# Head norm of three conv rows: a block-matrix mean, Ln and Exp on ScalarE and a Newton step on VectorE in place of group sums, a power on GpSimd and transposes

## What is computed

```python
proj = rms_norm(x, g_pre_mix) @ w_in                 # 3 x 512 conv and 3 x 512 attention columns
hc, bg, cg, q, k, v = split(proj, 6)
u = cg * hc
conv = bg * (u[s]*w2 + u[s-1]*w1 + u[s-2]*w0)        # causal, per channel, 512 channels
y_conv = conv * rsqrt(mean(conv*conv over each group of 64 channels) + 1e-6) * g_conv_out
y_attn = group_rms_norm(banded_attention(q, k, v), g_attn_out)
y = concat(y_conv, y_attn) @ w_out                   # then residual, norm, SwiGLU, residual
```

## Time and profile before

| | |
|---|---|
| time, median of 3 runs | 1108.63 us (1108.47 to 1108.7) |
| the profiled execution's own time | 1108.71 us |
| its span, first to last instruction | 1106.7 us |
| PE busy | 1096.9 us, 99% |
| DVE busy | 759.8 us, 69% |
| ACT busy | 467.3 us, 42% |
| POOL busy | 162.4 us, 15% |
| chain that ended last | PE 98%, ACT 1%, DVE 1% |
| mean granted clock of PE | 0.999 |

### The profile page before, as it was taken

The page is one execution under the profiler, slowest core; times in us unless marked ns, Lnnn a source line. Parts: engine busy times, 40 slices in busy tenths (PEclk is TensorE's granted clock), DMA queues, the critical chain, the costliest instruction groups (busy, mean ns, idle before and its releaser), DMA issues.

```text
span 1106.7 us, 15974 instructions
## 1 busy us (share of the span) xinstructions
PE 1096.9 (99%) x5653; PEld 909.5 (82%) x5653; DVE 759.8 (69%) x1206; ACT 467.3 (42%) x818; POOL 162.4 (15%) x258
## 2 busy tenths in 40 slices
PE   9999999999999999999999999999999999999997
PEld 7888888878888888888888888888888888888886
DVE  6878854354546656868787777878787786555584
ACT  6542333555555655734322232323223256444441
POOL 3300022010101220312112211211221110000031
PEclk9999999999999999999999999999999999999999
DMA  7332216300100444535546445543644689776632
GB/s 272 107 120 75 58 57 224 119 20 20 39 3 19 163 162 133 172 95 174 159 142 209 136 122 187 177 146 114 218 136 152 214 307 377 232 237 223 218 114 79
DMA packets 116182, 164.10 MB, mean 148 GB/s; under 512 B 7752, under 2 KB 73304, under 8 KB 116128
## 3 DMA queue, kind: packets, MB, share of 16 engines
q1 hardware_dynamic: 98496, 103.30, 29.3%
q0 software_dynamic: 16464, 55.89, 14.4%
q10 hardware_dynamic: 1168, 4.20, 1.0%
HBM read 119.56 MB, written 46.94 MB: 150 GB/s over the span
## 4 chain that ended last, share of the span: by engine, by line
PE 98%; ACT 1%; DVE 1%; DMA 0%; issue 0%; DVEq 0%; POOL 0%; POOLq 0%
PE psum L1278 34%; PE psum L1305 18%; PE psum L872 12%; PE psum L1111 10%; PE psum L1162 8%; PE psum L1023 4%; PE psum L915 3%; PE psum L896 2%; PE psum L886 2%; PE psum L861 1%; PE psum L999 1%; PE psum L923 0%; PE psum L1005 0%; PE psum L905 0%; ACT arena L1514 0%; PE psum L992 0%
## 5 line engine op out<-in xcount | busy, mean ns | idle before, releaser
L1278 PE MATMUL psum<-arena_r,ws 128*128 128x512 f32 x960 | 224.1, 389 | 0.0
L1278 PEld LDWEIGHTS psum<-arena_r,ws 128*128 128x128 f32 x960 | 180.3, 188 | 37.3
L1278 PE MATMUL psum<-hT,ws 128*128 128x512 f32 x720 | 169.9, 389 | 0.0
L1278 PEld LDWEIGHTS psum<-hT,ws 128*128 128x128 f32 x720 | 135.2, 188 | 27.9
L872 PE MATMUL psum<-hT,ws 128*128 128x512 f32 (+1 forms) x624 | 142.2, 380 | 0.6 <-ACT arena L1540 0.6
L1305 PE MATMUL psum<-hT 128*128 128x512 f32 (+1 forms) x600 | 135.2, 385 | 0.0
L1305 PEld LDWEIGHTS psum<-hT 128*128 128x128 f32 x600 | 111.3, 188 | 22.5
L872 PEld LDWEIGHTS psum<-hT,ws 128*128 128x128 f32 x624 | 107.9, 189 | 19.9 <-issue 0.8
L2408 DVE TENSOR_TENSOR misc<-misc,psum 128x512 f32<-128x512 f32 x100 | 68.6, 686 | 48.3 <-PE psum L1278 46.0
L1729 ACT ACTIVATE ws<-o_raw 128x512 fp32r<-128x512 f32 x40 | 25.1, 627 | 139.1 <-DVE o_raw L2386 138.6
L1162 PE MATMUL psum<-ws,hT 128*128 128x512 f32 x348 | 81.8, 393 | 0.0
(11 more groups left out here) (263 smaller groups left out, 1557.7 us busy)
## 6 DMA issues: line engine op xcount, KB each, us to landing
raw<-in_w_ffn_in SPq DMA_DIRECT2D x44, 512.0 KB, 4.2
act_scratch<-arena POOLq DMA_DIRECT2D x77, 256.0 KB, 3.2
raw<-in_w_in SPq DMA_DIRECT2D x22, 512.0 KB, 3.8
arena<-in_w_ffn_out POOLq DMA_DIRECT2D x22, 512.0 KB, 5.6
arena<-act_scratch SPq DMA_DIRECT2D x38, 256.0 KB, 3.3
arena<-in_x SPq DMA_DIRECT2D x16, 512.0 KB, 6.3
raw<-in_w_out SPq DMA_DIRECT2D x16, 512.0 KB, 3.4
raw<-act_scratch SPq DMA_DIRECT2D x26, 256.0 KB, 3.2
```

The source lines that it names most:

```text
L1278: last = mm(blocks(bank), w[:, k * P:(k + 1) * P], b_operand(i, part, k), start=fresh_bank and k == 0 and w is hi and part == 0, stop=k == ...
```

## The change

For rows 0 to 2 the means are made in channel layout. ACT squares the row into `CU` and makes its high part in `CR` (`high_sq`); DVE makes the low part (`low_sq`). PE multiplies both, in 512-column halves, by `same_head`, a 128x128 matrix with 1/64 where two channels share a group: 4 fp32r matmuls. Each of 128 partitions of `PP[2]` then holds its group's mean at each position. ACT takes Ln(mean + eps) and Exp(-0.5 x) of it (`conv_roots`), DVE does one Newton step on the inverse root and multiplies (`mix_row`), in four instructions over 1024 columns. POOL has no part in it any more, and the transposes and group sums of these rows are gone. `same_head` is filled once by ACT from `group`, in `high_sq(0)`.

```diff
             def stats(t):
 
-                pe.wait_ge(conv_sq, t + 1)
-                if t == 0:
-                    pe.wait_ge(v_copied, NT)
-                else:
-                    pe.wait_ge(conv_var, t)
-                conv_stats(PP[3]).then_inc(conv_stat, 1)
...
-            behind = {(4, 1): (stats, 0), (4, 3): (stats, 1), (4, 4): (norms, 0),
-                      (5, 0): (norms, 1), (5, 1): (stats, 2), (5, 4): (norms, 2)}
+                pe.wait_ge(conv_mixed, means_split(t))
+                if t > 0:
+                    pe.wait_ge(conv_mixed, mixed(t - 1))
+                for half in range(2):
+                    for part in (CR, CU):
+                        last = mm(PP[2][:, half * HALF:(half + 1) * HALF], same_head, row_r(part)[:, half * HALF:(half + 1) * HALF],
+                                  start=(part == CR), stop=(part == CU))
+                last.then_inc(conv_stat, 1)
+
+            behind = {(FRONT - 2, 3): 0, (FRONT - 1, 0): 1, (FRONT - 1, 3): 2}
...
+            def high_sq(t):
+
+                act.wait_ge(conv_sq, squared(t, 0))
...
+                if t > 0:
+                    act.wait_ge(conv_mixed, mixed(t - 1))
+                go(row_r(CR), row(CU), ACT.Copy).then_inc(conv_sq, 1)
+
+            def conv_roots(t, bank):
+
+                act.wait_ge(conv_stat, t + 1)
+                go(row(CR), bank, ACT.Ln, bias=eps_col[:, 0:1]).then_inc(conv_root, 1)
+                act.wait_ge(conv_root, rooted(t) - 1)
+                go(row(CR), row(CR), ACT.Exp, scale=-0.5).then_inc(conv_root, 1)
...
-            front_copy_first(4), square_y(0)
-            front_high(5, 0), square_y(1), front_high(5, 1), front_high(5, 2), front_high(5, 3)
-            spread_conv(0), front_high(5, 4), spread_conv(1), front_high(5, 6)
-            front_copy_first(5), square_y(2), front_high(5, 5)
+            front_copy_first(4), square_y(0), high_sq(0)
+            for i in range(4):
+                front_high(5, i)
+            conv_roots(0, PP[2]), square_y(1), front_high(5, 4), high_sq(1), front_high(5, 6)
+            front_copy_first(5), conv_roots(1, PP[2]), square_y(2), high_sq(2)
...
-            first_chunk(0), spread_conv(2)
+            first_chunk(0), front_high(5, 5), conv_roots(2, PP[2])
...
+            def low_sq(t):
+                dve.wait_ge(conv_sq, squared(t, 1))
+                tt(row_r(CU), row(CU), row_r(CR).bitcast(F32), ALU.subtract).then_inc(conv_mixed, 1)
+
+            def mix_row(t):
+
+                f, mean, y = row(CR), PP[2], row(CONV_ROWS[t])
+                dve.wait_ge(conv_root, rooted(t))
+                chain(stt(mean, mean, EPS, f, ALU.add, ALU.mult))
+                chain(stt(mean, mean, -0.5, f, ALU.mult, ALU.mult))
+                chain(stt(f, mean, 1.5, f, ALU.add, ALU.mult))
+                stt(y, y, params[:, t, 3:4], f, ALU.mult, ALU.mult).then_inc(conv_mixed, 1)
...
-            conv_stats_read(0)
+            low_sq(0)
             make_u3(4)
...
             front_low(5, 3)
+            mix_row(0)
             make_c22(4, tiles_of(row(CV), 1), 1)
-            conv_stats_read(1)
             front_low(5, 4)
+            low_sq(1)
             make_c21(4, tiles_of(row(CV), 0), 0)
-            conv_mix(0)
             front_low(5, 6)
             make_c12(4)
             times(2, 1, u2).then_inc(front_out, 1)
 
+            mix_row(1)
             make_u2(5)
-            conv_mix(1)
+            low_sq(2)
             make_u3(5)
-            conv_stats_read(2)
+            low(1, 0, 0)
             front_low(5, 5)
-            low(1, 0, 0)
+            mix_row(2)
             make_c22(5)
-            conv_mix(2)
```

More of the change, by code:

```diff
@@ L135, in trunk_layer @@
         arena_r = sb("arena_r", [P, NF * SEQ], F32R)
+        with nc.sbuf_tensor("misc_r", [P, 4 * BAND], F32R) as misc_r:
+            pass
         misc = sb("misc", [P, 4 * BAND])
@@ L138, in trunk_layer @@
         group = sb("group", [P, 2])
+        eps_col = sb("eps_col", [P, 1])
         params = sb("params", [P, PAIRS, 5])
@@ L242, in trunk_layer, with squared, rooted, means_split @@
         u2, u3, c22, s11, s4 = [misc[:, n * 512:(n + 1) * 512] for n in range(5)]
+        def squared(t, part):
+            return 2 * t + 1 + part
+        def rooted(t):
+            return 2 * t + 2
+        def means_split(t):
+            return 2 * t + 1
+        def mixed(t):
+            return 2 * t + 2
+        same_head = misc_r[:, 3 * 512:3 * 512 + P]
         s1, s2 = [o_raw[:, 4 * n:4 * n + 4, :].rearrange("p i c -> p (i c)") for n in range(2)]
@@ L411, in trunk_layer @@
         conv_norm = sem("conv_norm")
+        conv_root = sem("conv_root")
         conv_mixed = sem("conv_mixed")
@@ L569, in store_conv @@
             def store_conv(t):
-                sp.wait_ge(conv_mixed, t + 1)
+                sp.wait_ge(conv_mixed, mixed(t))
                 sp.dma_start(y_d[t * P:(t + 1) * P, :], row(CONV_ROWS[t])).then_inc(conv_stored[t], 16)
@@ L693, in _ @@
             pool.wait_ge(consts_made, 5)
+            nc.gpsimd.memset(eps_col[:, :], EPS).then_inc(consts_made, 1)
             chain = Chain(pool, pool_seq)
@@ L732, in conv_norm_factors @@
             def conv_norm_factors(t):
[L734 to L737, removed]
+                pool.wait_ge(conv_var, 1)
+                factors_to(crs[:, :], var[:, :], 16, conv_factors, 1)
             def o_norm_factors(t):
@@ L742, in o_norm_factors @@
                 factors_to(rst[:, :], o_eps[:, :], UNITS, o_rs, t + 1)
-            for t in range(PAIRS - 1):
-                conv_norm_factors(t)
             pool.wait_ge(prod, multiplied(FRONT - 1, 4))
@@ L969, in step @@
                     if s == 1 and t == 0:
-                        pe.wait_ge(conv_mixed, PAIRS - 1)
+                        pe.wait_ge(conv_mixed, mixed(LAST - 1))
                     if s == 2 and t > 1:
@@ L1116, in stats @@
             def stats(t):
-                pe.wait_ge(conv_sq, t + 1)
-                if t == 0:
-                    pe.wait_ge(v_copied, NT)
-                else:
-                    pe.wait_ge(conv_var, t)
-                conv_stats(PP[3]).then_inc(conv_stat, 1)
-            def norms(t):
-                pe.wait_ge(conv_rs, t + 1)
-                if t > 0:
-                    pe.wait_ge(conv_mixed, t)
-                conv_norms(PP[2], 0, NT).then_inc(conv_norm, 1)
-            behind = {(4, 1): (stats, 0), (4, 3): (stats, 1), (4, 4): (norms, 0),
-                      (5, 0): (norms, 1), (5, 1): (stats, 2), (5, 4): (norms, 2)}
+                pe.wait_ge(conv_mixed, means_split(t))
+                if t > 0:
+                    pe.wait_ge(conv_mixed, mixed(t - 1))
[5 more added lines that the diff above has]
+            behind = {(FRONT - 2, 3): 0, (FRONT - 1, 0): 1, (FRONT - 1, 3): 2}
             for n in range(FRONT):
@@ L1137, in _ @@
                     if (n, i) in behind:
-                        task, t = behind[n, i]
-                        task(t)
+                        stats(behind[n, i])
             for q in range(AHEAD):
@@ L1203, in _ @@
                     pe.wait_ge(oT_read, PAIRS)
-                    pe.wait_ge(conv_sq, PAIRS)
+                    pe.wait_ge(conv_sq, squared(LAST, 0))
                     conv_stats(PP[3]).then_inc(conv_stat, 1)
                 if c == 6:
-                    pe.wait_ge(conv_rs, PAIRS)
+                    pe.wait_ge(conv_rs, 1)
                     conv_norms(PP[3], 0, NT).then_inc(conv_norm, 1)
@@ L1458, in square_y, with spread_conv @@
                 go(row(CU), row(CONV_ROWS[t]), ACT.Square).then_inc(conv_sq, 1)
[L1460 to L1464, removed]
+            def high_sq(t):
+                act.wait_ge(conv_sq, squared(t, 0))
+                if t == 0:
+                    act.wait_ge(consts_made, 6)
+                    go(same_head.rearrange("p (g d) -> p g d", d=HD),
+                       group[:, :].rearrange("p (g o) -> p g o", o=1).broadcast_to([P, 2, HD]), ACT.Copy, scale=1.0 / HD)
+                if t > 0:
[6 more added lines that the diff above has]
+                go(row(CR), row(CR), ACT.Exp, scale=-0.5).then_inc(conv_root, 1)
+            def spread_conv():
+                act.wait_ge(conv_factors, 1)
                 go(row(CR).rearrange("p (g d) -> p g d", d=HD),
@@ L1700, in _ @@
                     act.wait_ge(oT_psum, PAIRS)
-                    spread_conv(PAIRS - 1)
+                    spread_conv()
                 for task, i in tasks.get(c, ()):
@@ L2331, in conv_last @@
             def conv_last(_):
-                dve.wait_ge(conv_norm, PAIRS)
+                dve.wait_ge(conv_norm, 1)
                 stt(row(PAIRS - 1), PP[3], params[:, LAST, 3:4], row(CV), ALU.mult, ALU.mult).then_inc(mix_done, 1)
```

## The result

The changed kernel takes 1124.91 us (median of 4 runs, 1124.46 to 1125.85) against 1108.59 us before (4 runs, 1108.47 to 1108.7). The ratio is 1.0148, 95% interval 1.0131 to 1.0166: 16.3 us slower. The forecast was 1123.7 us in a range of 1118 to 1130. The profiled execution took 1124.78 us, its span is 1122.9 us, the mean granted clock 0.991.

What follows compares the result with a forecast made beforehand. The prediction took PE as the bound: 16.75 us of new waits less 5.7 us of saved work gave +11.0, plus 4.0 for the clock, +15.0 on 1108.7, so 1123.7 us, range 1118 to 1130.

Steps and rivals of the forecast that it cites:

- What PE saves: PE, product (4, 1) to first piece: blocks replace three rows' group sums and transposes, gaining 5.7 us without any wait.
- A table load: ACT, around Ln and Exp of rows 0 to 2: six loads at 1.28 us each, plus 0.1 us lost overlap.
- the walk: Instruction lists laid on each other: PE waits 6.9, 4.0 and 5.85 us, 16.75 in all; less 5.7 gained, +11.0 us.
- The mix: DVE, each row: four dependent instructions in place of one, 4 x 1.32 = 5.3 us.
- The clock: PE after the waits of 6.9 and 5.85 us: slower clock costs 2 us each; the 4.0 us wait at 0.
- Queues and later stages: SP's stores ahead of k's weights and v's return come about as late as PE: 0; later stages have no slack.
- One sign missed: Profile sign: the distance from product (4, 1) to the first piece grows by 11 to 15 us, all else as before.
- A: Rival: the waits come as in the walk but PE's clock holds: 1119.7 us; chance 0.20.
- B: Rival: a table switch costs up to 1.4 us beyond each of six loads, 8.3 us: 1128 or 1132; chance 0.06.
- D: Rival: table loads are free beside ACT's other work, +4.3 us: 1113.0 us; chance 0.06.
- C: Rival: `mix_row` ends before PE needs what is queued behind it; 1103.0 us with all three waits gone; chance 0.04.

Runs made afterwards that it cites:

- e7: Changed kernel with ACT and DVE lists reordered, no Newton step, and Exp in place of Ln so no table loads: 1103.19 us, ratio 0.9953 to the kernel before.
- e4: Changed kernel with 60, 36 and 52 dummy transposes filling PE's three waits: 1120.35 us, ratio 1.0107 to the kernel before.
- e3: Changed kernel with the three Newton instructions of the mix left out: 1110.51 us, ratio 1.0019 to the kernel before.
- e2: Changed kernel with Ln replaced by Exp, so no table has to be loaded: 1116.16 us, ratio 1.0070 to the kernel before.
- e6: Changed kernel with ACT and DVE lists reordered and the three Newton instructions left out: 1104.93 us, ratio 0.9967 to the kernel before.
- e1: Changed kernel with the bank-emptying sums of rounds 4 and 5 ahead of the mixes on DVE: 1120.52 us, ratio 1.0106 to the kernel before.

## Why the prediction was right

- **What PE saves, 5.7 us.** Right: 5.4 us measured with a wait of 0.4 us left (e7). Blocks took 0.90 us.
- **A table load at 1.28 us.** Right: six loads of 1.28 us, in the order of the walk (the last starts at 186.79, a little behind the stretch that I gave, since the walk left the clock out), and the kernel without them is 8.75 us faster, clock included.
- **The mix, 4 x 1.32 us.** Slightly too high: 155.34 to 160.33 is 4.99 us. The three instructions of the Newton step took 1.23 us each and not 1.29. This is a part of why DVE as a whole got 13.8 us more and not the 16 that I worked out.
- **The walk.** Waits of 6.9, 4.0 and 5.85 us forecast, 6.72, 4.02 and 5.05 measured, each at the instruction named, behind the DVE line named. The third is shorter because product (5, 4) before it was slow; where it ran at full speed, in e4, the time before (5, 6) was 6.07 us.
- **The clock, 4 us.** The mechanism was right (granted clock at the lower level after the long waits, full speed in e4), and 4.6 us is its price by e4. The parts were not all right: I gave 0 to the wait of 4.0 us, with bounds of 0 to 1; it also dropped the clock and cost 0.8 us for the block on the path and 0.9 us that the next wait took in. The two priced at 2 us came to 1.9 and 2.0. That they came so close is luck: 2 us was the middle between bounds of 0 and 4, not a reading, and in e3 the same kernel paid in some runs and not in others. The rows behind the bounds were indirect as well. The windows view gives a granted clock of 1.00 for the first 10 us before the change, but only since the trace has no clock record before 9.01 us and the view counts such time as full. The spacing of the transposes bears the reading out: 0.21 us from start to start until 8.97 us, 0.11 from there on.
- **Queues and later stages, 0.** Right: 15.95 us late at the first scores and 16.2 us over the span.
- **One sign missed.** From product (4, 1) to the first piece I expected 11 to 15 us more; it is 16.1. Those bounds were the walk without and with 4 us for the clock, with no room for an error in either.
- **Rivals.** A is what e4 shows as a separate run, not the kernel itself. B and D are out by e2. C needed the mixes to end early; e6 gets there by leaving out three of four instructions and moving the one that is left.

Sum: 15.0 us forecast, 16.3 measured. Two errors partly cancel in the 1.3 us: the waits came to 1.0 us less than forecast (15.8 against 16.75), the lower clock to 1.6 us more (5.6 against 4.0); the rest, 0.4 us in the stretch and 0.2 behind it, I did not separate further. Not tried: keeping the Newton step and having it done elsewhere, or moving the blocks themselves. Nor do these runs say what the missing Newton step means for the accuracy of a use of e6.

## What to carry to other kernels

When an engine saves work on the bound, walk the new chain that replaces it, instruction by instruction against the queue in which each stands: here 5.7 us of PE work saved came with 15.8 us of waits, because two table loads and four dependent instructions on DVE stood in a chain that PE waited for, twice through a sum queued behind it. A long wait on PE should be priced above its length, since PE came back at half its clock, and what is won or lost there changes the next wait too. Moving the blocked instruction ahead only moves the wait while the chain is as long as before; shortening the chain and then ordering it is what made the kernel faster.

## What was not expected of the hardware

- Transposes of 128 columns, back to back at 0.11 us, kept the granted clock at 1.00 through stretches of 6.9, 4.2 and 6.1 us (e4), where it fell in or after the idle waits in the same places.
- The clock also fell after short waits, and not at every one of a size. In e3 a wait of 2.92 us was followed by a stretch at 0.76, in e1 one of 3.08 us by one at 1.00. Windows of these two runs, the wait and what follows it:

```profile
154.50:157.42 2.92, 0.00 (x1) 1.00 0.28 83
157.42:164.59 7.17, 7.17 (x24) 0.76 0.18 73
```

```profile
159.98:163.06 3.08, 0.00 (x1) 1.00 0.42 170
163.06:169.50 6.44, 6.44 (x28) 1.00 0.00 0
```

In both the clock stays up through the wait itself; in e3 it is down while PE works again.
- An operation of three operands on DVE over 1024 columns took 1.22 or 1.23 us where its scalar is a constant and 1.28 us where it is a column such as `params`; whether its operands lay in PSUM or in SBUF made less than 0.02 us. The trace before had such a row with a constant already, from the splitting of q, on operands in SBUF (busy us, mean ns of one):

```profile
L2172 DVE SCALAR_TENSOR_TENSOR ws<-arena,ws 128x1024 fp32r<-128x1024 f32 x3 | 3.7, 1217 | 0.0
```

It would have been the nearer row for the mix than the one of 1.29 us.
